# Two transformer blocks on one core: the value projections with 512-column matmuls into both accumulator banks

## The chip, the core and the metric

The kernel runs on one core of one Trainium2 chip. The metric is the device time of one launch in microseconds (us), from the first to the last instruction; lower is better. The core has a matrix engine (TensorE, PE in the profile, with a separate row PEld for its weight loads), a vector engine (VectorE, DVE), an activation engine (ScalarE, ACT), GpSimd (POOL), and SyncE (SP), which here only issues the DMAs of the weights and of input and output. Matmuls write their sums to PSUM, in banks of 128 partitions by 512 float32 values. Engines run their own instruction lists in order and wait for each other by semaphores.

## What is computed

One sequence of 256 tokens with 1024 features goes through two different blocks, all in float32. The first has block attention (8 heads of 64), gated linear attention (4 heads), and a gated feed-forward with a causal convolution; the second has a half-weighted feed-forward, two attentions (latent and chunked, 8 heads each), a gated merge, and another feed-forward. Cut to what bears on the change:

```python
proj = xn @ w_in[l]                                  # first block
mv = split_heads(proj[..., o_mv:o_gq], MOBA_HEADS)   # 512 columns of values
gv = split_heads(proj[..., o_gv:o_gr], GLA_HEADS)    # 512 columns of values
...
z = h @ w_in[l]                                      # second block
q_lat, kv_lat, k_pe_raw, ca_q, ca_k, ca_v, gate_a, gate_b = jnp.split(z, splits, axis=-1)
```

The three value projections `mv`, `gv` and `ca_v` (in the kernel `cav`) are each 256 tokens x 1024 features times 1024 x 512. Everything else that the kernel projects is needed with features on the partitions; the values are needed with tokens on the partitions, since attention sums over tokens.

## The kernel before

**Weights.** All weights arrive as one list of blocks of 128 x 1024 float32 (512 KB), called halves in the code; there are 282. SyncE loads half `h` into slot `h % 4` of `raw`. Each half is split into two float32r parts: ScalarE rounds it to `w_hi` (`hi`, L772), VectorE subtracts to get `w_lo` (`lo`, L1119). The activations `xn` are split alike into `xh` and `xl`. A product is then three matmuls: high x high, low x high, high x low. TensorE waits for `lo_ready` ahead of a half, and counts `half_used` up behind it; that count lets ScalarE overwrite the slot of the half four later, and tells it that a chunk of two halves is summed.

**Chunks.** A chunk is two halves, 256 weight columns by all 1024 features. It fills one PSUM bank. In the usual form (`feature_tile`, L355 to L357) the weights are the stationary operand and 256 tokens move. In the token form (`tokens_out=True`, L418 to L420) 128 tokens of `xh` or `xl` are stationary and 256 weight columns move; the two token halves fill the two halves of one bank. A half of either form is 24 matmuls of 256 columns. The token form is used for six chunks: 6 and 7 (`mv`), 8 and 9 (`gv`), `C_CAV` and `C_CAV + 1` (`cav`).

**Banks.** Chunks take PSUM banks 0 and 1 in turn (`bank_use(c)`). ScalarE empties a bank behind its chunk and counts `bank_free` up; TensorE waits for that count before it starts a new chunk in the bank. So one bank can be emptied while the next chunk fills the other.

**The order of the work.** Each engine's list is written out by hand. In the first block TensorE puts small pieces of attention between the halves: `rot` (rotary matmul), `level(l)` (one of nine steps of gated linear attention; it waits for `lv_q` from VectorE and `lv_k` from GpSimd, whose product is L298), `att_s`, `att_t`, `att_o` (scores, transposes, output of head pair `g`). From chunk 8 on, turn `g` of a loop runs the first half of chunk 8 + g, `att_s(g + 1)`, `att_t(g)`, `level(5 + g)`, the second half, `att_o(g)`. ScalarE's list in that turn is `hi` of a half, `att_pt`, `hi`, `att_exp(g + 1)`, `level_e`, `att_yh(g)` (L835, copies what `att_o` summed), and then the emptying of the chunk's bank (`vals`, L956, or `gr_evac`, L960).

In the second block TensorE runs a small projection into `v2` (L685 to L687; its two results lie in banks 1 and 0), then `C_CAV`, a rotary matmul (L704), `C_CAV + 1` with `s2(4)` (the scores of head pair 4) between its halves, and then eight chunks from `C_GATE` on with the attention pieces between the halves. ScalarE's list there: `hi` of `C_CAV`'s first half, the copy of `v2` from bank 1 (L1074), `hi` of the second half, the copy of `v2` from bank 0, `hi` of two halves, `vals` of `C_CAV`, `hi` of two halves, `att_exp(4)` (L826), `vals` of `C_CAV + 1`. `att_exp(4)` waits for `mask2(4)` on VectorE (L1274 to L1280), which waits for `s2(4)`.

`keep_clock` (L362) is a run of idle matmuls ahead of each norm's first chunk.

Of the kernel before, what the change touches and what calls it, by code (L numbers as in the profile page):

```python
# [19 lines left out]
P = 128  # L20
D = 1024
S = 256
KC = D // P
# [22 lines left out]
C_CAV = C_IN2 + 8  # L46
# [29 lines left out]
def build(nc, w, ada_w, x_in, cols_in, tab_in, gmask_in, glr_in, gup_in, bias_in, c_in, pos_in, out):  # L76
# [4 lines left out]
    ACT = mybir.ActivationFunctionType  # L81
# [3 lines left out]
    with ExitStack() as ctx:  # L85
# [114 lines left out]
        def slot(h):  # L200
            return h % NSLOT
# [150 lines left out]
        def _(pe):  # L352
# [11 lines left out]
            def feature_tile(u, h, kc, first, last):  # L364

                for f in range(2):
                    wc = slice((kc % 4) * 256 + f * P, (kc % 4) * 256 + f * P + P)
                    m = three(ps[:, u % 2, f * 256:f * 256 + 256], w_hi[:, slot(h), wc], w_lo[:, slot(h), wc],
                              xh[:, kc, :], xl[:, kc, :], first and f == 0, last)
                return m  # L370
# [26 lines left out]

            def chunk(c, i=0, tokens_out=False, halves=(0, 1)):

                ah, al = xh, xl  # L400
                u = bank_use(c)
                b = u % 2
                if halves[0] == 0 and not (isinstance(i, int) and u + 2 * i < 2):
                    pe.wait_ge(bank_free[b], u // 2 + i)
                for half in halves:
                    h = 2 * c + half
                    pe.wait_ge(lo_ready, h + 1 + 4 * i)
                    for k in range(4):
                        kc = 4 * half + k
                        first, last = half == 0 and k == 0, half == 1 and k == 3  # L410
                        if not tokens_out:
                            m = feature_tile(u, h, kc, first, last)
                            continue
                        for f in range(2):
                            a = slice(f * P, f * P + P)
                            wcol = slice(k * 256, k * 256 + 256)
                            o = ps[:, b, f * 256:f * 256 + 256]
                            pe.matmul(o, ah[:, kc, a], w_hi[:, slot(h), wcol], start=first and f == 0, stop=False, skip_group_check=True)  # L418
                            pe.matmul(o, al[:, kc, a], w_hi[:, slot(h), wcol], start=False, stop=False, skip_group_check=True)  # L419
                            m = pe.matmul(o, ah[:, kc, a], w_lo[:, slot(h), wcol], start=False, stop=last, skip_group_check=True)  # L420
                    m.then_inc(half_used, 1)
# [159 lines left out]
            level(1)  # L581
            chunk(6, tokens_out=True, halves=(0,))
            rot(5)
            level(2)
            chunk(6, tokens_out=True, halves=(1,))
            chunk(7, tokens_out=True, halves=(0,))
            level(3)
            chunk(7, tokens_out=True, halves=(1,))
            pe.wait_ge(rope_done, 4)
            att_s(0, b1["qT"], b1["kz"])  # L590
            level(4)
            for g in range(4):
                c = 8 + g
                chunk(c, tokens_out=c < 10, halves=(0,))
                if g < 3:
# [4 lines left out]
                else:  # L600
                    pe.wait_ge(lv_copied, 17)
                    evacuated(pe, 9)
                    for h in range(4):
# [5 lines left out]
                        if h % 2:  # L609
                            m.then_inc(go_full, 1)  # L610
                chunk(c, tokens_out=c < 10, halves=(1,))
                if g == 0:
# [87 lines left out]

            chunk(C_CAV, tokens_out=True, halves=(0,))
            evacuated(pe, bank_use(C_UQ) + 2)
            pe.wait_ge(pe_done, 1)
            pe.matmul(ps[:, 3, :], table("perm32", P), b2["qpr"][:, :], start=True, stop=True).then_inc(pe_rot, 1)  # L704
            chunk(C_CAV, tokens_out=True, halves=(1,))
            chunk(C_CAV + 1, tokens_out=True, halves=(0,))
            pe.wait_ge(pe_done, 2)
            evacuated(pe, bank_use(C_UQ) + 3)
            evacuated(pe, bank_use(C_UQ) + 4)
            s2(4)  # L710
            chunk(C_CAV + 1, tokens_out=True, halves=(1,))
            for c in range(8):
# [41 lines left out]
        def _(act):  # L754
# [198 lines left out]

            def vals(dst, c, cc):
                b = full(c)
                f(dst[:, :, cc * 256:cc * 256 + 256], bank2(b), ACT.Copy).then_inc(bank_free[b], 1)  # L956

# [5 lines left out]
            for c in range(2, 6):  # L963
                qraw(c)
                hi(c + 2)
                level_e(c - 2)
            vals(b1["mv"], 6, 0)
            hi(8)
            level_e(4)
            vals(b1["mv"], 7, 1)  # L970
            level_e(5)
            att_exp(0, sm1, st1)
            for g in range(4):
# [16 lines left out]
                if g == 3:  # L990
                    hi(C_OUT1 + 1, halves=(0,))
                if g < 2:
                    vals(b1["gv"], c, g)
                else:
                    gr_evac(c, g - 2)
# [79 lines left out]
            hi(C_CAV + 1)  # L1075
            vals(b2["cav"], C_CAV, 0)
            hi(C_GATE)
            att_exp(4, b2["sm2"], b2["st2"])
            vals(b2["cav"], C_CAV + 1, 1)
            for c in range(8):  # L1080
# [541 lines left out]
def _weights(a):  # L1622
# [11 lines left out]
    w = a["w_in"][0]  # L1634

    for c0, n in ((1536, 256), (1792, 256), (0, 512), (512, 512), (1024, 512), (2048, 512), (2560, 512)):
        for c in range(c0, c0 + n, 256):
            feature_chunk(w, r(c, c + 256))
# [17 lines left out]
    s.append(_padded(s[-1][:, :0]))  # L1656
    for c in range(1440, 4000, 256):
        feature_chunk(w, r(c, c + 256))
# [74 lines left out]
```

## Time and profile before

| what | before |
|---|---|
| device time, median of 3 runs | 1019.54 us (1017.79 to 1022.6) |
| span of the profiled execution | 1017.8 us |
| TensorE busy | 947.2 us (93%), 7412 matmuls |
| VectorE, ScalarE, GpSimd busy | 73%, 53%, 33% |
| the 288 matmuls of the value projections (L418 to L420) | 28.4, 27.1 and 27.1 us, about 283 ns each |
| DMA | 191.57 MB, mean 188 GB/s |

The profiled execution is one execution; its span stands beside the lowest of the three runs and 1.7 us under their median. A matmul's duration of about 283 ns covers its whole way through the engine; matmuls overlap, so their cost in a stream is the distance between the starts of two of them, which only the rows in order of time show. "Idle before" in a row is how long the engine had been without work, and the arrow names what ended it.

### The profile page before, as it was taken

The numbers are of one execution on the slowest core, as the hardware profiler recorded it, in microseconds if no ns is written. First come the engines' busy times: TensorE is split into PE (matmuls) and PEld (weight loads), VectorE is DVE, ScalarE is ACT, GpSimd is POOL, SyncE is SP. The second block draws the span as 40 slices with busy tenths as digits, with TensorE's granted clock in tenths as the row PEclk, the third lists the DMA queues.
The fourth block names the chain that finished last, engine by engine and source line by source line (L and its number), as shares of the span: only waits on it lengthen the run. The fifth ranks groups of instructions, "written<-read, shape, count | busy, mean of one in ns | idle before, by whom it ended". The sixth has DMA issues, their size and how long they took to land.

```text
span 1017.8 us, 20346 instructions
## 1 busy us (share of the span) xinstructions
PE 947.2 (93%) x7412; PEld 909.2 (89%) x7412; DVE 747.9 (73%) x942; ACT 539.5 (53%) x846; POOL 334.1 (33%) x267
## 2 busy tenths in 40 slices
PE   7999999888888986999997998999999999999996
PEld 5889998878888986899997997989999999999996
DVE  4589766999999666799999678666667575656444
ACT  4635566765656552665655455555554454343432
POOL 2053203656656883288656665000000000000000
PEclk9999999999999997999999899999999999999999
DMA  6443346767767775388886753553345546555651
GB/s 225 128 132 114 104 144 213 243 214 225 226 217 225 268 275 192 99 281 278 284 274 228 277 190 130 189 188 102 112 135 168 167 147 185 174 188 174 208 164 42
DMA packets 53228, 191.57 MB, mean 188 GB/s; under 512 B 5921, under 2 KB 6305, under 8 KB 53057
## 3 DMA queue, kind: packets, MB, share of 16 engines
q1 hardware_dynamic: 41760, 149.96, 45.1%
q0 software_dynamic: 10704, 39.46, 12.1%
q10 hardware_dynamic: 720, 1.54, 0.4%
q8 instruction: 31, 0.51, 0.2%
q14 instruction: 13, 0.10, 0.0%
HBM read 189.89 MB, written 1.05 MB: 188 GB/s over the span
## 4 chain that ended last, share of the span: by engine, by line
PE 64%; DVE 13%; issue 11%; POOL 5%; ACT 3%; DMA 1%; DVEq 1%; POOLq 0%; SPq 0%; ACTq 0%
PE ps L355 18%; PE ps L356 17%; PE ps L357 17%; POOL ada_mul L317 4%; DVE w_lo L1119 3%; PE ps L443 2%; PE ps L493 2%; DVE act_hi L1375 1%; DMA raw<-w 1%; PE ps L429 1%; DVE cv L1358 1%; DVE rstd L1124 1%; PE ps L418 1%; PE ps L419 1%; PE ps L420 1%
## 5 line engine op out<-in xcount | busy, mean ns | idle before, releaser
L355 PE MATMUL ps<-xh,w_hi 128*128 128x256 f32 x1472 | 424.8, 289 | 31.1 <-DVE w_lo L1119 21.3
L1119 DVE TENSOR_TENSOR w_lo<-raw,w_hi 128x1024 fp32r<-128x1024 f32 x282 | 368.1, 1331 | 116.2 <-ACT w_hi L772 115.9
L356 PE MATMUL ps<-xl,w_hi 128*128 128x256 f32 x1472 | 418.2, 284 | 0.0
L357 PE MATMUL ps<-xh,w_lo 128*128 128x256 f32 x1472 | 418.2, 284 | 0.0
L772 ACT ACTIVATE w_hi<-raw 128x1024 fp32r<-128x1024 f32 x282 | 286.7, 1052 | 76.2 <-PE ps L357 70.8
L355 PEld LDWEIGHTS ps<-xh,w_hi 128*128 128x128 f32 x1472 | 284.1, 193 | 41.0 <-DVE w_lo L1119 29.6
L356 PEld LDWEIGHTS ps<-xl,w_hi 128*128 128x128 f32 x1472 | 284.3, 193 | 0.3 <-issue 0.2
L357 PEld LDWEIGHTS ps<-xh,w_lo 128*128 128x128 f32 x1472 | 284.0, 193 | 0.0
L317 POOL TENSOR_TENSOR ada_mul<-ada_raw,cact 128x1024 f32<-128x1024 f32 x72 | 189.4, 2631 | 8.8 <-ACT cact L1010 8.8
L355 PE MATMUL ps<-act_hi,w_hi 128*128 (+1 forms) x528 | 153.1, 290 | 24.3 <-DVE w_lo L1119 24.3
L356 PE MATMUL ps<-act_lo,w_hi 128*128 (+1 forms) x528 | 150.9, 286 | 0.0
L357 PE MATMUL ps<-act_hi,w_lo 128*128 (+1 forms) x528 | 150.6, 285 | 0.0
L355 PEld LDWEIGHTS ps<-act_hi,w_hi 128*128 128x128 f32 x528 | 102.6, 194 | 26.0 <-issue 24.1
L356 PEld LDWEIGHTS ps<-act_lo,w_hi 128*128 128x128 f32 x528 | 102.7, 194 | 0.2
L357 PEld LDWEIGHTS ps<-act_hi,w_lo 128*128 128x128 f32 x528 | 102.4, 194 | 0.0
L1377 DVE TENSOR_TENSOR act_lo<-av,act_hi 128x256 f32 (+1 forms) x66 | 88.5, 1340 | 7.6
L310 POOL COPY mod<-ada_col 128x1 f32 (+1 forms) x72 | 55.5, 771 | 112.5 <-ACT ada_mul L878 112.3
L878 ACT ACTIVATE ada_mul<-ada_mul 128x1024 f32<-128x1024 f32 x72 | 75.5, 1049 | 28.3 <-POOL ada_mul L317 28.3
L869 ACT ACTIVATE sg<-ps 128x256 f32<-128x256 f32 x44 | 16.9, 383 | 123.5 <-PE ps L357 123.5
L303 POOL DMA_DIRECT2D ada_raw<-ada_w x72 | 42.3, 588 | 42.9 <-POOL ada_mul L317 41.6
L298 POOL TENSOR_TENSOR KL<-gkz,E 128x512 f32<-128x512 f32 x16 | 28.8, 1824 | 76.1 <-ACT E L847 76.1
L1375 DVE CAST act_hi<-av 128x256 f32 (+1 forms) x66 | 49.9, 755 | 0.0
(245 smaller groups left out, 1086.0 us busy)
## 6 DMA issues: line engine op xcount, KB each, us to landing
raw<-w SPq DMA_DIRECT2D x282, 512.0 KB, 4.3
ada_raw<-ada_w POOLq DMA_DIRECT2D x72, 512.0 KB, 4.1
X<-x_in SPq DMA_DIRECT2D x4, 256.0 KB, 5.8
bm<-bias_in POOLq DMA_DIRECT2D x1, 1024.0 KB, 5.2
out<-X SPq DMA_DIRECT2D x4, 256.0 KB, 2.2
tab<-tab_in ACTq DMA_DIRECT2D x1, 640.0 KB, 8.1
gmask<-gmask_in ACTq DMA_DIRECT2D x1, 512.0 KB, 10.2
cact<-c_in POOLq DMA_DIRECT2D x1, 512.0 KB, 5.1
```

The lines of the kernel that those rows point to most:

```text
L298: ins = pool.tensor_tensor(b1["KL"][:, l % 2, par, :, :], b1["gkz"][:, par, :, :], b1["E"][:, l % 2, :, :], ALU.mult)
L303: pool.dma_start(ada_raw[:, k, :], src).then_inc(ada_landed[k], 16)
L310: pool.tensor_copy(mod_cols[:, ds(n, 1)], ada_col[:, k:k + 1]).then_inc(ada_moved, 1)
L317: pool.tensor_tensor(ada_mul[:, k % 2, :], ada_raw[:, k, :], cact[:, :], ALU.mult).then_inc(ada_mult, 1)
L355: pe.matmul(o, lh, rh, start=start, stop=False, skip_group_check=True)
L356: pe.matmul(o, lh, rl, start=False, stop=False, skip_group_check=True)
L357: return pe.matmul(o, ll, rh, start=False, stop=stop, skip_group_check=True)
L772: f(w_hi[:, slot(h), :], raw[:, slot(h), :], ACT.Copy).then_inc(hi_ready, 1)
L878: f(ada_mul[:, n % 2, :], ada_mul[:, n % 2, :], ACT.Copy, accum_out=ada_col[:, n % 2:n % 2 + 1]).then_inc(ada_used, 1)
L1119: v.tensor_tensor(w_lo[:, slot(h), :], raw[:, slot(h), :], w_hi[:, slot(h), :].bitcast(F32), ALU.subtract).then_inc(lo_ready, 1)
L1375: v.tensor_copy(ah, av[:, vv, :]).then_inc(ah_done, 1)
L1377: v.tensor_tensor(al, av[:, vv, :], ah.bitcast(F32), ALU.subtract).then_inc(act_ready, 1)
```

## The change

The two chunks of a value projection become one piece of work, `wide(c, quarters)`. A half of its weights now holds two feature blocks (of 128) by 512 columns, not four by 256; the list of weights on the host is laid out so (`token_chunk`). A quarter is one such half: 12 matmuls of 512 columns, six for each token half, and token half `t` has a whole bank, `(bank_use(c) + t) % 2`. Both banks are filled throughout all four quarters. `wide` waits for both banks before its first quarter. The quarters stand where the four halves stood, with the same pieces of attention between them.

On ScalarE `vals(dst, c)` now empties both banks behind the fourth quarter, with two copies of 128 x 512. For `mv` it comes at the place of the second `vals`, and `hi(8)` and `level_e(4)` keep their order; for `gv` it comes in turn g = 1; for `cav` behind `att_exp(4)`.

```diff
+            def wide(c, quarters):
+                u = bank_use(c)
+                if quarters[0] == 0:
+                    for j in range(2):
+                        pe.wait_ge(bank_free[(u + j) % 2], (u + j) // 2)
+                for q in quarters:
+                    h = 2 * c + q
+                    pe.wait_ge(lo_ready, h + 1)
+                    for k in range(2):
+                        kc = 2 * q + k
+                        first, last = kc == 0, kc == KC - 1
+                        wcol = slice(k * 512, k * 512 + 512)
+                        for t in range(2):
+                            a = slice(t * P, t * P + P)
+                            o = ps[:, (u + t) % 2, :]
+                            pe.matmul(o, xh[:, kc, a], w_hi[:, slot(h), wcol], start=first, stop=False)
+                            pe.matmul(o, xl[:, kc, a], w_hi[:, slot(h), wcol], start=False, stop=False)
+                            m = pe.matmul(o, xh[:, kc, a], w_lo[:, slot(h), wcol], start=False, stop=last)
+                    m.then_inc(half_used, 1)
...
-            chunk(6, tokens_out=True, halves=(0,))
+            wide(6, (0,))
             rot(5)
             level(2)
-            chunk(6, tokens_out=True, halves=(1,))
-            chunk(7, tokens_out=True, halves=(0,))
+            wide(6, (1, 2))
             level(3)
-            chunk(7, tokens_out=True, halves=(1,))
+            wide(6, (3,))
...
-                chunk(c, tokens_out=c < 10, halves=(0,))
+                if g < 2:
+                    wide(8, (2 * g,))
+                else:
+                    chunk(c, halves=(0,))
...
-            chunk(C_CAV, tokens_out=True, halves=(0,))
+            wide(C_CAV, (0,))
...
-            chunk(C_CAV, tokens_out=True, halves=(1,))
-            chunk(C_CAV + 1, tokens_out=True, halves=(0,))
+            wide(C_CAV, (1, 2))
...
             s2(4)
-            chunk(C_CAV + 1, tokens_out=True, halves=(1,))
+            wide(C_CAV, (3,))
...
-            def vals(dst, c, cc):
-                b = full(c)
-                f(dst[:, :, cc * 256:cc * 256 + 256], bank2(b), ACT.Copy).then_inc(bank_free[b], 1)
+            def vals(dst, c):
+                full(c + 1)
+                for t in range(2):
+                    b = (bank_use(c) + t) % 2
+                    f(dst[:, t, :], ps[:, b, :], ACT.Copy).then_inc(bank_free[b], 1)
...
-            vals(b1["mv"], 6, 0)
             hi(8)
             level_e(4)
-            vals(b1["mv"], 7, 1)
+            vals(b1["mv"], 6)
...
-                if g < 2:
-                    vals(b1["gv"], c, g)
-                else:
+                if g == 1:
+                    vals(b1["gv"], 8)
+                elif g >= 2:
                     gr_evac(c, g - 2)
...
-            vals(b2["cav"], C_CAV, 0)
             hi(C_GATE)
             att_exp(4, b2["sm2"], b2["st2"])
-            vals(b2["cav"], C_CAV + 1, 1)
+            vals(b2["cav"], C_CAV)
```

Three places of the instruction lists follow. Line numbers of the changed kernel differ from those of the kernel before.

On TensorE, where `C_CAV` begins, behind the last three matmuls of the `v2` projection. Before:

```order
L685 MATMUL ps<-w_hi,cqh 128x512 [waits bank0_free]
L686 MATMUL ps<-w_hi,cql 128x512
L687 MATMUL ps<-w_lo,cqh 128x512
L418 MATMUL ps<-w_hi,xh 128x256 [waits lo_ready,bank1_free]
L419 MATMUL ps<-w_hi,xl 128x256
L420 MATMUL ps<-w_lo,xh 128x256
```

And in the changed kernel:

```order
L701 MATMUL ps<-w_hi,cqh 128x512 [waits bank0_free]
L702 MATMUL ps<-w_hi,cql 128x512
L703 MATMUL ps<-w_lo,cqh 128x512
L414 MATMUL ps<-w_hi,xh 128x512 [waits lo_ready,bank0_free,bank1_free]
L415 MATMUL ps<-w_hi,xl 128x512
L416 MATMUL ps<-w_lo,xh 128x512
```

The first matmul of the projection waited for bank 1 alone; now it waits for bank 0 too, which the `v2` matmuls right ahead of it have just filled.

On ScalarE, from the copies of `v2` to those of `cav` (`w_hi<-raw` is `hi` of one half, `sm2` with its sums `st2` is `att_exp(4)`). Before:

```order
L1074 ACTIVATE v2<-ps 128x512
L772 ACTIVATE w_hi<-raw 128x1024
L1074 ACTIVATE v2<-ps 128x512
L772 ACTIVATE w_hi<-raw 128x1024 x2
L956 ACTIVATE cav<-ps 128x2x256
L772 ACTIVATE w_hi<-raw 128x1024 x2
L826 ACT_TABLE_LOAD
L826 ACTIVATE sm2,st2<-sm2,st2 128x128 x2
L826 ACTIVATE sm2,st2<-sm2,st2 128x256 x2
L956 ACTIVATE cav<-ps 128x2x256
```

And in the changed kernel:

```order
L1091 ACTIVATE v2<-ps 128x512
L787 ACTIVATE w_hi<-raw 128x1024
L1091 ACTIVATE v2<-ps 128x512
L787 ACTIVATE w_hi<-raw 128x1024 x4
L841 ACT_TABLE_LOAD
L841 ACTIVATE sm2,st2<-sm2,st2 128x128 x2
L841 ACTIVATE sm2,st2<-sm2,st2 128x256 x2
L974 ACTIVATE cav<-ps 128x512 x2
```

The first copy of `cav` moved from ahead of the exponentials to behind them; both banks are now emptied there.

On ScalarE, from turn g = 0 to turn g = 1 of the loop in the first block (`yh1` is `att_yh`, `pt1` is `att_pt`). Before:

```order
L835 ACTIVATE yh1<-ps 128x256
L956 ACTIVATE gv<-ps 128x2x256
L772 ACTIVATE w_hi<-raw 128x1024
L831 ACTIVATE pt1<-ps 128x512
L772 ACTIVATE w_hi<-raw 128x1024
L826 ACTIVATE sm1,st1<-sm1,st1 128x128 x2
L826 ACTIVATE sm1,st1<-sm1,st1 128x256 x2
L845 ACTIVATE E<-E 128x512
L847 ACTIVATE E<-E 128x512
L835 ACTIVATE yh1<-ps 128x256
L956 ACTIVATE gv<-ps 128x2x256
```

And in the changed kernel:

```order
L850 ACTIVATE yh1<-ps 128x256
L787 ACTIVATE w_hi<-raw 128x1024
L846 ACTIVATE pt1<-ps 128x512
L787 ACTIVATE w_hi<-raw 128x1024
L841 ACTIVATE sm1,st1<-sm1,st1 128x128 x2
L841 ACTIVATE sm1,st1<-sm1,st1 128x256 x2
L860 ACTIVATE E<-E 128x512
L862 ACTIVATE E<-E 128x512
L850 ACTIVATE yh1<-ps 128x256
L974 ACTIVATE gv<-ps 128x512 x2
```

The copy at the end of turn 0 is gone, and the one at the end of turn 1 has become two.

## Rows read from the trace of the kernel before

**Rows 1.** The page: engine totals, and the granted TensorE clock in 40 slices.
```profile
PE 947.2 (93%) x7412; PEld 909.2 (89%) x7412; DVE 747.9 (73%) x942; ACT 539.5 (53%) x846; POOL 334.1 (33%) x267
PEclk9999999999999997999999899999999999999999
```
**Rows 2.** Stretches: us, busy time of each engine, clock, DMA share, GB/s.
```profile
68.00:110.00 42.00, 42.00 (x340) 39.91 (x340) 38.86 (x66) 22.73 (x49) 14.34 (x9) 1.00 0.29 93
674.00:790.00 116.00, 115.74 (x930) 110.06 (x930) 78.83 (x138) 62.12 (x128) 0.00 (x0) 1.00 0.43 140
```
**Rows 3.** TensorE in order of time: start, duration; 256 columns (first, last of 23), 512 (first, last of 5).
```profile
70.38 0.28 PE L419 MATMUL ps<-w_hi,xl 128*128 128x256 f32 x1
...
73.01 0.28 PE L420 MATMUL ps<-w_lo,xh 128*128 128x256 f32 x1
...
671.47 0.39 PE L686 MATMUL ps<-w_hi,cql 128*128 128x512 f32 x1
...
672.40 0.40 PE L687 MATMUL ps<-w_lo,cqh 128*128 128x512 f32 x1
```
**Rows 4.** TensorE and ScalarE at the starts of chunks 6 and 8.
```profile
70.18 0.36 PE L418 MATMUL ps<-w_hi,xh 128*128 128x256 f32 x1
...
67.82 0.60 ACT L952 ACTIVATE qraw<-ps 128x512 f32<-128x512 f32 x1 [5.20 <-PE ps L357]
...
89.45 0.36 PE L418 MATMUL ps<-w_hi,xh 128*128 128x256 f32 x1
...
86.55 0.60 ACT L956 ACTIVATE mv<-ps 128x512 f32<-128x512 f32 x1 [4.03 <-PE ps L420]
```
**Rows 5.** GpSimd's product for level 6, and TensorE's matmuls of level 6.
```profile
100.06 4.31 POOL L298 TENSOR_TENSOR KL<-gkz,E 128x512 f32<-128x512 f32 x2 [8.95 <-ACT E L847]
...
104.85 1.90 PE L493 MATMUL ps<-QL,KL 128*128 128x64 f32 x16
```
**Rows 6.** TensorE and ScalarE at the end of turn 1 and the start of chunk 10.
```profile
110.07 0.40 PE L469 MATMUL ps<-pt,mv 128*64 128x128 f32 x4
110.39 0.39 PE L355 MATMUL ps<-xh,w_hi 128*128 128x256 f32 x1
...
110.80 0.60 ACT L956 ACTIVATE gv<-ps 128x512 f32<-128x512 f32 x1
```
**Rows 7.** The start of C_CAV: TensorE, ScalarE, VectorE.
```profile
674.26 0.36 PE L418 MATMUL ps<-w_hi,xh 128*128 128x256 f32 x1 [1.46 <-DVE w_lo L1119]
...
674.32 0.59 ACT L1074 ACTIVATE v<-ps 128x512 f32<-128x512 f32 x1
...
672.89 1.22 DVE L1119 TENSOR_TENSOR w_lo<-raw,w_hi 128x1024 fp32r<-128x1024 f32 x1 [0.62 <-ACT w_hi L772]
```
**Rows 8.** From s2(4) to the first chunk of C_GATE: TensorE, ScalarE.
```profile
689.19 0.28 PE L420 MATMUL ps<-w_lo,xh 128*128 128x256 f32 x1
689.31 0.28 PE L355 MATMUL ps<-xh,w_hi 128*128 128x256 f32 x1
...
688.82 0.40 ACT L826 ACTIVATE sm<-sm,st 128x128 f32<-128x128 f32 x1 [3.89 <-DVE st L1280]
...
690.59 0.57 ACT L956 ACTIVATE cav<-ps 128x512 f32<-128x512 f32 x1
```
**Rows 9.** TensorE after idle stretches, and the clock granted after two of them.
```profile
178.88 0.39 PE L355 MATMUL ps<-xh,w_hi 128*128 128x256 f32 x1 [1.63 <-DVE w_lo L1119]
...
340.45 0.56 PE L355 MATMUL ps<-act_hi,w_hi 128*128 x1 [1.90 <-DVE w_lo L1119]
...
343.81 0.33 PE L355 MATMUL ps<-act_hi,w_hi 128*128 x1
...
178.90:182.30 3.40, 3.40 (x28) 3.40 (x29) 2.13 (x5) 3.40 (x10) 0.90 (x2) 1.00 0.88 289
340.40:343.80 3.40, 3.35 (x15) 3.35 (x16) 3.40 (x2) 1.90 (x2) 3.40 (x3) 0.51 0.75 264
```
**Rows 10.** All waits: engine, line <- what ended it: us in total, times, longest.
```profile
POOL cact L323 <- PE ps L357: 47.0, 1, 47.0
```

More of the change, by code:

```diff
@@ L396, in first_two, with chunk @@
                     m.then_inc(half_used, 1)
-            def chunk(c, i=0, tokens_out=False, halves=(0, 1)):
-                ah, al = xh, xl
+            def wide(c, quarters):
[17 more added lines that the diff above has]
+                    m.then_inc(half_used, 1)
+            def chunk(c, i=0, halves=(0, 1)):
                 u = bank_use(c)
@@ L410, in chunk @@
                         first, last = half == 0 and k == 0, half == 1 and k == 3
[L411 to L420, printed above, removed]
+                        m = feature_tile(u, h, kc, first, last)
                     m.then_inc(half_used, 1)
@@ L610, in _ @@
                             m.then_inc(go_full, 1)
-                chunk(c, tokens_out=c < 10, halves=(1,))
+                if g < 2:
+                    wide(8, (2 * g + 1,))
+                else:
+                    chunk(c, halves=(1,))
                 if g == 0:
@@ L1634, in _weights, with token_chunk @@
     w = a["w_in"][0]
+    def token_chunk(w, c):
+        s.extend([_tiles(w, k, 2, c) for k in range(0, KC, 2)])
     for c0, n in ((1536, 256), (1792, 256), (0, 512), (512, 512), (1024, 512), (2048, 512), (2560, 512)):
+        if c0 in (1024, 2048):
+            token_chunk(w, r(c0, c0 + 512))
+            continue
         for c in range(c0, c0 + n, 256):
@@ L1656, in _weights @@
     s.append(_padded(s[-1][:, :0]))
-    for c in range(1440, 4000, 256):
+    token_chunk(w, r(1440, 1952))
+    for c in range(1952, 4000, 256):
         feature_chunk(w, r(c, c + 256))
```

## The prediction

> **What bounds the kernel now.** I read the engine totals first [rows 1]: TensorE is busy 93% of the span, VectorE 73%. Then the two stretches in which the value projections lie [rows 2]: TensorE is busy for all 42.0 us of the first and 115.74 of 116.0 us of the second, at the full clock. The reader should see that an edit here is paid by TensorE's own list, matmul by matmul, and that each new wait on it is paid too. VectorE is close behind in the first stretch (38.86 of 42.0 us), so there a faster TensorE may run into it or into what it feeds. Last come the rows in order of time around each place where the change waits for a bank.
>
> **The matmuls.** 288 matmuls of 256 columns become 144 of 512. The 283 ns of one is no price, since they overlap; the starts are. At 256 columns, 23 starts take 73.01 - 70.38 = 2.63 us, 0.1195 us each. At 512 columns, in float32r with the same three products, the first and the last of five starts are 672.40 - 671.47 = 0.93 us apart, 0.2325 us each [rows 3]. Two narrow ones cost 0.239 to 0.240, one wide one 0.2325. So a wide one saves 0.007 us, a half of 24 narrow matmuls saves 12 x 0.007 = 0.085 us, and the 12 halves save 1.0 us in all. What the weight loads cost at either width is in these distances already, so their halved count brings nothing beyond that. That is the whole gain that the trace supports. The rest of the change is about when two banks must be free.
>
> The Trainium skill ("TensorE: Matmul & The Clock Gate", Back-to-back issue gap) puts a sustained stream of weight loads and matmuls at about 81 ns for 128 columns and 131 ns for 512. Interpolated to some 98 ns at 256, a pair would save about 65 ns, an estimate of 9.4 us for 144 pairs. The rows show 232.5 ns at 512 columns where that page has 131, so the sum goes by the rows.
>
> **Chunk 6, covered.** `wide(6)` needs the bank of chunk 5, which `qraw` empties from 67.82 to 68.42; TensorE comes at 70.18 [rows 4]. The matmuls of `rot` and `level(1)` hide it, with 1.8 us to spare. Nothing.
>
> **Chunk 8, covered.** `wide(8)` needs both banks of `mv`. The single copy ran at 86.55, for 0.60 us; a second one follows about 0.5 later and ends near 87.65, and TensorE comes at 89.45 [rows 4]. `att_s(0)` and `level(4)` hide it. Without them it would cost some 1.2 us. ScalarE has `level_e(5)` half a microsecond later, which TensorE needs only a whole half and two pieces of attention later.
>
> **Level 6, a part of the gain lost.** TensorE has saved seven halves, 0.60 us, when it comes to level 6, which began at 104.85. GpSimd's product for it ended at 100.06 + 4.31 = 104.37 [rows 5]; it starts from VectorE's and ScalarE's chain, which is not moved. With 0.10 for the semaphore TensorE can start at 104.47, so only 0.38 of the 0.60 remain. With the eighth half the first block's gain is 0.46 us.
>
> **Chunk 10, a new wait.** Chunk 10 used the bank that `vals` had emptied a turn earlier. Now it is emptied in turn 1, behind `att_yh(1)`, which waits for `att_o(1)`, the work right ahead of chunk 10. The copy ran from 110.80 to 111.40 [rows 6]. From a finished release to the first matmul I take 0.14 us, from the start of `C_CAV` (674.12 to 674.26, [rows 7]). So chunk 10 starts at 111.54, not at 110.39: 1.15 us, all on TensorE, with chunk 11, the output projection and everything behind queued after it. The second copy delays `hi` of a half that TensorE needs a half and some attention later: nothing. First block: +1.15 - 0.46 = **+0.7 us**.
>
> **C_CAV, a longer wait.** Before, TensorE waited here 1.46 us for `w_lo` (672.89 + 1.22). Now it needs the second copy of `v2` too, which stands behind `hi` of a half and ends at 674.32 + 0.59 = 674.91; with 0.14 the start is 675.05, not 674.26 [rows 7]: **+0.8 us**. `w_lo` of the later halves stays ahead.
>
> **C_GATE, the largest wait.** TensorE ended the projection and went on at 689.31 without a stop, since that bank had been emptied ahead of the exponentials. Now both copies stand behind `att_exp(4)`, and that waits for VectorE's mask, which waits for `s2(4)`. `s2(4)` moves by 0.79 for `C_CAV`'s late start and back by three halves, 0.25: +0.54. The exponentials ran from 688.82 to 690.59, and a copy takes 0.57 [rows 8]. So the first bank is free at 690.59 + 0.54 + 0.57 = 691.70, and TensorE goes on at 691.84, not 689.31: +2.5 us, which holds the +0.8 of `C_CAV` and the gain of the four halves (0.34) in it. Behind it wait the eight gate chunks with all attention, and through them the rest. If the exponentials ran before TensorE was done, the cost would be one copy and a semaphore, 0.7 in place of about 2.1; they can't, since `s2(4)` has to come ahead of them. Second block: **+2.5 us**.
>
> The Trainium skill ("Perfetto Trace Analysis", Matmuls) says that independent groups should rotate through the banks, so that the emptying of one overlaps the next, and also that larger matmuls are more efficient. The change trades the first for the second. By the rule alone each of the five starts would pay a copy, about 0.6 us, so 3.0 in all; the rows put two of them at nothing and one at over 2.
>
> **The clock.** TensorE's idle stretches get longer. An idle stretch of 1.63 us was followed by a full clock; one of 1.90 was followed by one of half speed (0.51, 1.2 of 2.4 GHz) until 343.81 [rows 9]. There the 16 starts from 340.45 on took 3.36 us, where the full clock takes 16 x 0.12 = 1.92: 1.45 us lost. After the change TensorE is idle from 672.80 (672.40 + 0.40, [rows 3]) to 675.05, 2.25 us, longer than the row that lost its clock, and from about 689.9 to 691.8, 1.9 us, which equals it. I take one loss of the two: **+1.45 us**; the ends are none and 2.9.
>
> **The sum.** +0.7 + 2.5 + 1.45 = +4.65 us. Does any of it get hidden later? The one long chain apart from TensorE's is GpSimd's modulation product, and it starts from a TensorE matmul behind the first new wait [rows 10]; all norms start from TensorE too. So it stays. Against the profiled execution, 1017.8 + 4.65 = 1022.5; that execution stands at the low end of the three runs, and for the median I take 1019.54 + 4.65 = **1024.2 us**.
>
> **The rivals.**
> Both stretches lose the clock (slower by over 0.5%). The place is the same, the price a second 1.45 us, and it decides from an idle stretch between 1.63 and 1.90 us on: +6.1, 1025.6. For it: both idle stretches reach 1.90. Against: one equals it only just, and the idle ends are worked out to a tenth at best.
> No clock is lost: +3.2, 1022.7. For it: the only row of this length is a single one.
> The waits cost nothing (faster, or the same). That would be so if TensorE's delay ran into a later wait that didn't move, as at level 6. The 1.0 or 0.7 us gain is left: 1018.6. Against: TensorE idles 0.26 us in the 116 us behind `C_CAV` [rows 2].
> The wide matmul is much cheaper than its five starts show, because those stood in a run of six only. The bound is that it costs one narrow start: 144 x 0.12 = -17 us; halfway, and less the waits, about 1012. Against: the four distances are equal to a hundredth. The skill's figures above are this rival.
> The change doesn't do what it says: the lists show 512 columns and both waits, so I give that nothing.
>
> **How the numbers follow.** One clock loss 0.36, both 0.24, none 0.24, waits hidden wholly or for the most part 0.10, cheap wide matmul 0.02, the rest for what I have not seen. The range 1019.8 to 1026.6 takes the first three with 1 us either way for the runs' own spread. A measurement of this kernel tells about 0.5%, 5.1 us, from no change, which is 1024.6. Slower: both losses and some 0.3 of the single one, 0.36. Faster: 0.04, the cheap matmul with a little more. Same: 0.60.
>
> **What would show it.** In the changed profile: wide starts 0.2325 apart; no idle stretch ahead of chunks 6 and 8; one of about 1.1 us ahead of chunk 10, released by a `gv` copy; 2.2 ahead of `C_CAV`, released by a `v2` copy; 1.9 ahead of `C_GATE`, released by a `cav` copy behind the exponentials; half clock behind one of the last two. I am wrong if starts are under 0.22, if the copy ahead of `C_GATE` comes before the exponentials, or if the difference at 690 is not found again at the end.

## The result, and the profile after

| what | before | changed |
|---|---|---|
| device time, median | 1019.38 us (1017.72 to 1022.6, 20 runs) | 1022.99 us (1019.86 to 1026.81, 20 runs) |
| ratio to before | | 1.0036, 95% interval 1.0024 to 1.0048 |
| span of the profiled execution | 1017.8 us | 1024.4 us |
| matmuls | 7412 | 7268 |

The changed kernel is 3.7 us slower (2.4 to 4.9), inside the half per cent that was called no change. One run of the kernel before, of 1144.2 us at a mean clock of 0.75, is left out of everything below. Line numbers below are those of the changed kernel, or of the kernel that is named.

The page of the changed kernel has TensorE's busy time up by 1.4 us, though it has 144 matmuls fewer, and the clock row has other notches than before [rows 1]:

```profile
PE 948.6 (93%) x7268; PEld 903.6 (88%) x7268; DVE 751.6 (73%) x942; ACT 539.4 (53%) x846; POOL 333.3 (33%) x267
...
PEclk8989999999999998999998999999999999999998
```

The list of all waits of TensorE (us in total, times, longest) names the new ones:

```profile
PE ps L414 <- ACT v L1091: 2.2, 1, 2.2
...
PE ps L355 <- ACT cav L974: 1.8, 1, 1.8
...
PE ps L355 <- ACT gv L974: 1.0, 1, 1.0
...
PE ps L504 <- DVE AT L1357: 0.3, 1, 0.3
```

The first three are ahead of `C_CAV`, `C_GATE` and chunk 10. The fourth, ahead of level 3, was not forecast. In order of time, with the idle time before each and what ended it:

```profile
84.34 1.97 PE L504 MATMUL ps<-QL,KL 128*128 128x64 f32 x16 [0.30 <-DVE AT L1357]
...
113.80 0.39 PE L355 MATMUL ps<-xh,w_hi 128*128 128x256 f32 x1 [0.98 <-ACT gv L974]
...
677.75 0.47 PE L414 MATMUL ps<-w_hi,xh 128*128 128x512 f32 x1 [2.21 <-ACT v L1091]
...
694.33 0.54 PE L355 MATMUL ps<-xh,w_hi 128*128 128x256 f32 x1 [1.85 <-ACT cav L974]
```

The last three answer to [rows 6 to 8], where `C_CAV` alone waited, for 1.46 us. The wide matmuls themselves, in the second and third quarter of `cav`, the first and the last of 21 starts:

```profile
682.13 0.40 PE L414 MATMUL ps<-w_hi,xh 128*128 128x512 f32 x1
...
686.70 0.40 PE L416 MATMUL ps<-w_lo,xh 128*128 128x512 f32 x1
```

20 distances in 4.57 us are 0.2285 us each, against 0.2325 in [rows 3] and 0.239 for two narrow ones. That is the price inside a stream; what a whole quarter saves comes with the experiments.

**Where the 6.6 us between the two profiled executions lie.** Both traces are cut at the same starts of TensorE: the first matmul of chunk 6, of chunk 10, of the `v2` projection, of `C_CAV`, of `C_GATE`, and of the transposes of head pair 4.

| stretch | before | changed | difference |
|---|---|---|---|
| start to chunk 6 | 70.18 | 72.91 | +2.73 |
| chunk 6 to chunk 10 | 40.21 | 40.89 | +0.68 |
| chunk 10 to `v2` | 560.77 | 560.10 | -0.67 |
| `v2` to `C_CAV` | 3.10 | 3.85 | +0.75 |
| `C_CAV` to `C_GATE` | 15.05 | 16.58 | +1.53 |
| `C_GATE` to the transposes | 5.50 | 7.10 | +1.60 |
| transposes to the end | 322.99 | 322.97 | -0.02 |

The first row can't come from the change, which begins at chunk 6. There and in the third row the two executions differ in where the clock was at half speed. The three rows of the change itself, 0.68 + 0.75 + 1.53 = **2.96 us**, are the banks and the matmuls. The sixth row is the clock behind the wait for `cav`:

```profile
677.80:681.00 3.20, 3.20 (x13) 2.48 (x14) 2.99 (x3) 1.85 (x2) 0.00 (x0) 1.00 0.79 221
694.30:697.60 3.30, 3.27 (x15) 3.27 (x16) 1.98 (x5) 1.41 (x2) 0.00 (x0) 0.52 0.00 0
```

(Stretch, length, busy time of PE, PEld, DVE, ACT, POOL, granted clock, DMA share, GB/s.) Behind the 2.21 us wait the clock stayed at 2.4 GHz, behind the 1.85 us wait it was at 1.2 GHz.

### The profile page after: what moved, and what is told of

Same layout as the page of the kernel before. It is cut to its first block, busy times and chain, and to the rows that moved or that the text cites. A ratio compares the mean times of both kernels' runs of the same rounds, so it can differ in the third digit from the quotient of the medians.

```text
span 1024.4 us, 20055 instructions
## 1 busy us (share of the span) xinstructions
PE 948.6 (93%) x7268; PEld 903.6 (88%) x7268; DVE 751.6 (73%) x942; ACT 539.4 (53%) x846; POOL 333.3 (33%) x267
## 4 chain that ended last, share of the span: by engine, by line
PE 65%; DVE 14%; issue 12%; POOL 4%; ACT 3%; DMA 1%; DVEq 1%; POOLq 0%; SPq 0%; ACTq 0%
PE ps L355 18%; PE ps L356 18%; PE ps L357 18%; POOL ada_mul L317 3%; DVE w_lo L1135 2%; PE ps L454 2%; PE ps L440 1%; PE ps L504 1%; DVE cv L1374 1%; DVE rstd L1140 1%; DVE cv L1371 1%; DMA raw<-w 1%; ACT w_hi L787 1%; DVE av L1379 1%; DVE act_hi L1391 1%
## 5 line engine op out<-in xcount | busy, mean ns | idle before, releaser
L1393 DVE TENSOR_TENSOR act_lo<-av,act_hi 128x256 f32 (+1 forms) x66 | 94.9, 1438 | 7.6
L1386 DVE TENSOR_TENSOR av<-sg,ps 128x256 f32<-128x256 f32 x44 | 18.3, 416 | 39.8 <-ACT sg L884 39.5
```

The lines of the kernel that those rows point to most:

```text
L1393: v.tensor_tensor(al, av[:, vv, :], ah.bitcast(F32), ALU.subtract).then_inc(act_ready, 1)
```

## The experiments

Since one execution differs from the next by where its clock falls, I read three things of each kernel: the stretches between the starts above, from its profile; the ratio to the kernel before; and the difference at equal clock. For the last, 246 runs (each has its time and its mean granted clock) were fitted with one slope and one level per kernel; the slope is 0.59 us for 0.001 of the clock. Its intervals are 95%, but the runs come from several chips: with a level for each chip as well, the values move by up to 0.5 us (cav_bank2 to +0.4, mv_copy_first to +0.3, all_four to -0.5). Nor does equal clock take out all that the clock costs. By estimate, a loss of 3.2 us at half speed lowers the mean clock of a run by 0.0016, which the slope values at 0.9 us, where the traces below have it cost 1.5 to 1.6. So a kernel that often loses its clock behind a wait keeps a part of that price in the last column.

| kernel | chunk 6 to 10 | `v2` to `C_CAV` | `C_CAV` to `C_GATE` | ratio (95%) | at equal clock, us |
|---|---|---|---|---|---|
| before | 40.21 | 3.10 | 15.05 | 1 | 0 |
| changed | 40.89 | 3.85 | 16.58 | 1.0036 (1.0024 to 1.0048) | +4.0 ± 0.4 |
| mv_only | 40.19 | 3.10 | 15.05 | 1.0005 (0.999 to 1.0021) | +0.3 ± 0.5 |
| gv_only | 40.84 | 3.09 | 15.05 | 1.0 (0.9985 to 1.0015) | +0.8 ± 0.5 |
| cav_only | 40.20 | 3.84 | 18.17 (clock lost) | 1.0021 (1.0006 to 1.0036) | +2.6 ± 0.5 |
| all_three | 39.80 | 3.00 | 14.72 | 0.9987 (0.9972 to 1.0002) | -0.9 ± 0.5 |
| gv_first | 39.80 | 3.84 | 16.58 | 1.0039 (1.0022 to 1.0056) | +2.4 ± 0.5 |
| cav_first | 40.88 | 3.85 | 16.99 (clock lost) | 1.0025 (1.0006 to 1.0043) | +2.4 ± 0.5 |
| cav_bank2 | 40.87 | 3.00 | 14.70 | 0.9995 (0.9978 to 1.0013) | +0.8 ± 0.5 |
| longer | 40.89 | 3.85 | 18.97 (clock lost) | 1.0043 (1.0024 to 1.0063) | +5.3 ± 0.6 |
| mv_copy_first | 40.20 | 3.10 | 15.05 | 0.9987 (0.9968 to 1.0005) | -0.1 ± 0.5 |
| before_copy_first | 40.22 | 3.10 | 15.05 | 0.9997 (0.9976 to 1.0017) | -0.2 ± 0.5 |
| all_four | 39.78 | 3.00 | 14.70 | 0.9995 (0.9978 to 1.0011) | -1.0 ± 0.5 |

The theory under test: the loss is three waits for banks, one ahead of chunk 10, two around `cav`, and the clock behind the longer ones. Its rivals: the wide matmuls cost something of their own; or one of the two blocks makes the loss alone.

### One projection at a time

```diff
 mv_only (gv and cav as before):
-                if g < 2:
-                    wide(8, (2 * g,))
-                else:
-                    chunk(c, halves=(0,))
+                chunk(c, tokens_out=c < 10, halves=(0,))
...
-            wide(C_CAV, (0,))
+            chunk(C_CAV, tokens_out=True, halves=(0,))
```

The other quarters, the copies of ScalarE and the layout of the weights go back in the same way; in gv_only and cav_only it is the other two projections that do.

> Only the mv projection is wide; gv and cav stay as two chunks. Theory of the waits: no idle stretch of TensorE ahead of chunks 6 and 8, four quarters 0.085 us shorter each, so -0.3 us against the kernel before. Rival (wide matmuls themselves bring a cost that the waits don't show): TensorE is idle ahead of chunk 6 or 8, or the stretch from chunk 6 to chunk 8 is not shorter.

> Only the gv projection is wide. Theory of the waits: TensorE is idle about 1.0 us ahead of chunk 10, released by the copy of gv; level 6 is not held, since only three quarters are saved ahead of it; +1.15 - 0.34 = +0.8 us. Rival (the wait is made up by a later one): the idle stretch is there, but the time from chunk 10 to the first norm is shorter by as much.

> Only the cav projection is wide. Theory of the waits: idle stretches of 2.2 us ahead of C_CAV and 1.9 ahead of C_GATE, +2.5 us from L685 to C_GATE, and in most executions one or two losses of the clock of 1.45 us, so +2.5 to +5.4, about +3.5 in the median. Rival (the first block's waits make the loss): under +1.5.

gv_only and cav_only have the waits that were expected, at slightly lower prices. gv_only loses 40.84 - 40.21 = 0.63 us (0.8 expected), with 0.98 us of idle ahead of chunk 10. cav_only's ratio is 2.1 us (0.6 to 3.7), under the 2.5 to 5.4 that were expected. It loses 0.74 ahead of `C_CAV`, and then has both waits, with the clock lost behind the first this time and kept behind the second:

```profile
675.45 0.67 PE L414 MATMUL ps<-w_hi,xh 128*128 128x512 f32 x1 [2.21 <-ACT v L1100]
675.92 0.63 PE L415 MATMUL ps<-w_hi,xl 128*128 128x512 f32 x1
676.35 0.63 PE L416 MATMUL ps<-w_lo,xh 128*128 128x512 f32 x1
...
693.62 0.38 PE L355 MATMUL ps<-xh,w_hi 128*128 128x256 f32 x1 [1.85 <-ACT cav L978]
693.85 0.28 PE L356 MATMUL ps<-xl,w_hi 128*128 128x256 f32 x1
693.97 0.28 PE L357 MATMUL ps<-xh,w_lo 128*128 128x256 f32 x1
```

Starts 0.43 us apart at the first place are half speed; 0.12 at the second is full speed. `C_CAV` to `C_GATE` took 18.17 us here and 16.58 where the clock stayed: 1.59 us for one loss. At equal clock the three parts add up to 0.3 + 0.8 + 2.6 = 3.7 us, the changed kernel has 4.0. So two thirds of the loss are `cav`; by the stretches it is 2.28 of 2.96 us, three quarters.

mv_only did not give its gain: 40.19 us, where 39.9 was expected. Its trace has TensorE held ahead of level 3, not by a bank of chunks, but by VectorE's copy of level 2 (`level_copy(2)`, L1366 there):

```profile
83.50 0.74 PE L513 MATMUL ps<-QL,KL 128*128 128x64 f32 x5 [0.31 <-DVE AT L1366]
```

So what failed is not the banks. There was no idle ahead of chunks 6 and 8, as the theory had it, but chunk 6 to chunk 8 took 19.26 us against 19.27 before: not shorter, which was the second of the rival's two signs. Whether wide matmuls cost something of their own, as the rival said, or VectorE takes the gain, mv_only alone can't tell; the experiments below can.

### The waits taken away

all_three:

```diff
+                if g == 1:
+                    vals(b1["gv"], 8)
                 att_yh(g, yh1, g)
...
-                    for j in range(2):
+                    for j in range(2 if c != C_CAV else 0):
                         pe.wait_ge(bank_free[(u + j) % 2], (u + j) // 2)
...
-                            o = ps[:, (u + t) % 2, :]
+                            o = ps[:, 2 if c == C_CAV and t == 0 else (u + t) % 2, :]
+                            if c == C_CAV and kc == 0 and t == 1:
+                                pe.wait_ge(bank_free[(u + 1) % 2], (u + 1) // 2)
```

ScalarE copies `cav`'s first half from bank 2 without counting `bank_free`, and its first copy of `v2` counts two, since bank 1 then stays free. cav_bank2 has these edits without the first one, gv_first has the first one alone.

> All three projections wide, with the waits taken away: the copies of gv stand ahead of att_yh(1); token half 0 of cav is summed in bank 2, which is free there, so that C_GATE finds its bank empty, and the wait for bank 0 stands ahead of the first matmul of token half 1. Theory of the waits: no idle stretch ahead of chunk 10 and C_GATE, 1.5 ahead of C_CAV as before; -0.7 to -1.0 us against the kernel before, so 1018.5 or so. Rival (wide matmuls cost something of their own, or the clock falls in any case): it stays at +1 or more.

> The changed kernel with token half 0 of cav in bank 2 and the wait for bank 0 ahead of the first matmul of token half 1; gv as in the changed kernel. Theory: no idle ahead of C_GATE, 1.5 ahead of C_CAV; against the kernel before only the first block's +0.7 is left, less 0.34: +0.4 us. Rival: the stretch behind C_CAV still is longer than before.

> The changed kernel with the copies of gv ahead of att_yh(1) on ScalarE; all else alike. Theory: the first copy runs while TensorE is in att_o(1), so the 1.0 us of idle ahead of chunk 10 shrinks to under 0.2, and nothing else moves: 1.0 us less than the changed kernel. Rival (att_yh(1), now 1.1 us later, is waited for): the same time turns up ahead of a later matmul of attention.

In their stretches all three came out by the theory. all_three takes 39.80, 3.00 and 14.72 us where the kernel before takes 40.21, 3.10 and 15.05: 0.84 us less. (0.10 of that is a start of `C_CAV` that comes sooner behind the same release; no row says why.) The time agrees: -0.9 us at equal clock, while the ratio, 0.9987 (0.9972 to 1.0002), doesn't exclude no change. With all_four below, this is the fastest form of the change, by a gain that can only just be told.

The quarters show what the wide form saves where it stands. The four halves of `gv` took 11.99 us before and 11.54 in all_three, those of `cav` 12.16 and 11.84. The saving is 0.45 and 0.32 us, about 0.1 per quarter and not the 12 x (0.239 - 0.2285) = 0.13 of the long stream: in a quarter by itself the starts are 0.23 apart. The last quarter of `cav`, before and in all_three, the first two starts and the gate's:

```profile
686.25 0.47 PE L418 MATMUL ps<-w_hi,xh 128*128 128x256 f32 x1
686.55 0.28 PE L419 MATMUL ps<-w_hi,xl 128*128 128x256 f32 x1
...
689.31 0.28 PE L355 MATMUL ps<-xh,w_hi 128*128 128x256 f32 x1
...
685.12 0.58 PE L416 MATMUL ps<-w_hi,xh 128*128 128x512 f32 x1
685.54 0.39 PE L417 MATMUL ps<-w_hi,xl 128*128 128x512 f32 x1
...
688.08 0.28 PE L355 MATMUL ps<-xh,w_hi 128*128 128x256 f32 x1
```

The quarter took 3.06 and 2.96 us; behind the first distance, 11 wide ones take 2.54 us, 0.231 each. So the wide form has no cost of its own that would eat the gain, and the gain is there once nothing waits.

In cav_bank2 TensorE goes from `cav` to the gate chunks without a stop:

```profile
691.77 0.39 PE L418 MATMUL ps<-w_lo,xh 128*128 128x512 f32 x1
692.00 0.28 PE L355 MATMUL ps<-xh,w_hi 128*128 128x256 f32 x1
...
693.39 0.57 ACT L976 ACTIVATE cav<-ps 128x512 f32<-128x512 f32 x1
```

The copy ends at 693.96, two microseconds behind the gate's first matmul, and nobody waits. cav_bank2 keeps only the first block's loss. Its stretches add up to 0.66 - 0.10 - 0.35 = +0.2 us where +0.4 was expected; at equal clock it is +0.8 ± 0.5, and its ratio, 0.9995, shows no difference. In gv_first the copies ran ahead of `att_yh`, the first of them while TensorE was in `att_o(1)`, and chunk 6 to chunk 10 fell from 40.89 to 39.80. The time behind it, chunk 10 to the output projection, is 21.98 us in gv_first and 21.97 in the changed kernel, so the later `att_yh` is waited for by no one. Its ratio, 1.0039, is not under the changed kernel's; two kernels measured apart are told from each other to 0.2% at best, and at equal clock it is 1.6 us lower.

### The order of the copies around the exponentials, and a longer wait

```diff
 cav_first:
-            att_exp(4, b2["sm2"], b2["st2"])
             vals(b2["cav"], C_CAV)
+            att_exp(4, b2["sm2"], b2["st2"])
...
 longer:
             att_exp(4, b2["sm2"], b2["st2"])
+            f(b2["th"][:, 0:4, :], b2["bm"][:, 0:4, :], ACT.Copy)
             vals(b2["cav"], C_CAV)
```

> The changed kernel with the copies of cav ahead of att_exp(4); all else alike. Theory: TensorE waits for one copy and a semaphore ahead of C_GATE, some 0.7 us and not 1.85, and the exponentials end 1 us later, which transpose 4 doesn't need yet: 1.2 us less than the changed kernel, and no clock loss at C_GATE, up to 1.45 more in executions that had one. Rival (the exponentials are late then): an idle stretch ahead of the transposes of head pair 4.

> The changed kernel with one more copy of 128 x 1024 on ScalarE (into a tile that is overwritten later) between att_exp(4) and the copies of cav. Theory: the wait ahead of C_GATE is on the path in full, so it grows from 1.85 to 2.9 us and the time by 1.05, and at 2.9 us idle the clock falls behind it in nearly every execution, which adds some 0.7 in the median: +1.0 to +2.5 against the changed kernel. Rival (delays here are made up later): less than 0.5.

cav_first: the idle ahead of `C_GATE` fell from 1.85 to 0.69 us:

```profile
687.91 0.39 PE L355 MATMUL ps<-xh,w_hi 128*128 128x256 f32 x1 [0.69 <-ACT cav L974]
```

`C_CAV` to `C_GATE` is 16.99 us, against 18.17 in cav_only; both lost the clock behind `C_CAV`. That is 1.18 us less, as expected, and `C_GATE` to the transposes is 5.59 us, so the late exponentials are hidden. longer: the idle grew to 2.79 us, and the stretch to 18.97, 0.80 more than cav_only's (`cav`'s last quarter with the wait behind it took 5.91 us against 4.96, 0.95 more; the loss of clock in the first quarter cost 0.14 less). The clock was lost behind both waits, and the transposes came 7.09 us behind `C_GATE` instead of 5.6. At equal clock it is 1.3 us over the changed kernel, by the ratios 0.7. The delay is not made up. So the wait ahead of `C_GATE` is paid in full, and what sets its length is the row of work that stands between `s2(4)` and the copy.

### What holds mv's gain

```diff
 mv_copy_first (mv_only with), before_copy_first (before with), all_four (all_three with):
+            level_copy(2)
             level_d(4)
-            level_copy(2)
```

> Only mv wide, as in mv_only, and on VectorE level_copy(2) stands ahead of level_d(4). In mv_only TensorE was idle 0.31 us ahead of level 3, released by that copy, and the stretch from chunk 6 to chunk 10 was 40.19 us against 40.21 before. Theory (VectorE's copy takes the gain of mv): the copy ends 0.6 us earlier, the idle stretch is gone and chunk 6 to chunk 10 takes 39.85 to 39.9. Rival (wide quarters of mv save nothing there for another reason): 40.2 with no idle stretch, or the wait turns up at level 4.

> The kernel before with the same two VectorE instructions swapped and nothing wide. Theory: the copy hardly held TensorE there, so chunk 6 to chunk 10 takes 40.1 to 40.2 and the time is the same. Rival (the swap is worth something by itself): 39.9 or less.

> All three projections wide, the three waits taken away as in all_three, and the swap on VectorE. Theory: chunk 6 to chunk 10 takes 39.45 to 39.5 (39.80 in all_three), and the whole is 1.0 to 1.4 us under the kernel before at equal clock. Rival (level 6 holds it now, by GpSimd's product): 39.7 to 39.8, with an idle stretch ahead of level 6.

The copy that held level 3 came earlier, and that wait went. But the gain did not come: 40.20 us, and the wait is at level 4 now, for VectorE's next copy, as the rival said. all_four shows the same, 39.78 us with no wait at level 6, so neither of the two forecasts for that stretch holds; its -1.0 ± 0.5 us at equal clock is just at the edge of the 1.0 to 1.4 that were expected. On VectorE in mv_copy_first:

```profile
86.27 1.97 PE L513 MATMUL ps<-QL,KL 128*128 128x64 f32 x16 [0.48 <-DVE AT L1366]
...
79.04 0.76 DVE L1366 COPY_PREDICATED AT<-gmask,ps 128x256 f32<-128x256 int32 x2
79.71 0.69 DVE L1337 TENSOR_TENSOR E<-G 128x512 f32<-128x512 f32 x1
80.31 2.36 DVE L1144 TENSOR_TENSOR w_lo<-raw,w_hi 128x1024 fp32r<-128x1024 f32 x2
82.58 1.52 DVE L1343 TENSOR_TENSOR QL<-gq,E 128x256 f32<-128x256 f32 x1
84.03 1.76 DVE L1337 TENSOR_TENSOR E<-G 128x512 f32<-128x512 f32 x1
85.71 0.75 DVE L1366 COPY_PREDICATED AT<-gmask,ps 128x256 f32<-128x256 int32 x2
```

and around level 4, where VectorE's busy time is the third figure behind the length:

```profile
82.00:90.00 8.00, 7.52 (x51) 6.65 (x50) 7.96 (x11) 3.88 (x11) 5.96 (x4) 1.00 0.37 131
```

VectorE is busy for 7.96 of 8.0 us around level 4. In this stretch its list is as long as TensorE's, so whatever TensorE saves on `mv` it waits for at the next level. Which level that is depends on the order; the sum does not. All thirteen kernels show it, wide or narrow, swapped or not: VectorE's copy of level 3 starts 16.90 to 16.93 us behind the start of chunk 6, level 4 on TensorE 17.47 to 17.50, and chunk 6 to chunk 8 takes 19.25 to 19.28 us. The copy, in the kernel before (chunk 6 at 70.18) and in mv_only (at 72.07):

```profile
87.10 0.76 DVE L1341 COPY_PREDICATED AT<-gmask,ps 128x256 f32<-128x256 int32 x2
...
88.98 0.76 DVE L1366 COPY_PREDICATED AT<-gmask,ps 128x256 f32<-128x256 int32 x2
```

The kernel before stood at that edge already: chunk 6 to chunk 10 is 40.21 there and 40.22 with the swap. And it is not the wide form that costs `mv` its gain: in all_four its second and third quarter, with no wait among them, took 5.55 us against 5.84 for the same halves in before_copy_first, and level 3 began 10.97 us behind chunk 6 against 11.35. Level 4 began at 17.49 and 17.50: the gain was there, and was waited for.

## Why the prediction was right, point by point

**The waits, found and placed.** All three were where the prediction had them, released by what it named. Chunks 6 and 8 had no idle ahead of them.

**The clock.** Taken: one loss of 1.45 us. A loss costs 1.59 behind `C_CAV` and 1.50 behind `C_GATE` (7.10 - 5.60), so the price was near. How often it happens was read from one row, and there the forecast was too high for the median: of the 3.7 us, 2.96 are the three stretches, so about 0.7 (-0.6 to +1.9) is left for the clock. In the five profiles that have both waits (changed, cav_only, gv_first, longer, and cav_first, whose second wait is only 0.69), a 2.2 us wait lost the clock in three and kept it in two; a 1.85 us wait lost it in one of three; the 2.79 us wait lost it. An idle stretch of this length loses the clock in some executions and not in others. Both ends of the range, none and two, do occur: gv_first had none, longer had both.

**The matmuls.** Forecast 0.085 us per half, from 0.2325 us a start. The long stream in the middle of `cav` has 0.2285, but the quarters of the changed kernel that stand alone have 0.229 to 0.238 behind their first distance, with [rows 3]'s 0.2325 in the middle. The quarters of `gv` and `cav` save 0.77 us in eight, 0.10 each, so this term held. The rival of a much cheaper matmul is out: it saved 0.0105 us, not 0.12. (That rival's 1012 us left out most of the waits: 1019.5 - 8.6 for the matmuls + 1.15 + 2.9 for the waits is some 1015.)

**Level 6.** This step of the prediction failed. TensorE was to be held by GpSimd's product there; it was held by VectorE's copy at level 3, and chunk 6 to chunk 8 kept its length to 0.01 us. So all of `mv`'s gain was lost, 0.5 us by its quarters in all_four, and not 0.2. TensorE began level 3 11.43 us behind chunk 6 in the changed kernel and 11.44 before, level 4 17.48 and 17.49: it was held at both. The sign stood in the trace of before: VectorE busy for 38.86 of 42.0 us [rows 2], which the prediction read and then followed up at the wrong engine.

**Chunk 10.** Forecast +1.15 for the wait. From the end of `gv`'s last quarter to chunk 10 the changed kernel took 1.86 us and the kernel before 0.80, so the wait cost 1.06. The 0.1 less is the release: the first copy ended at 113.75 (113.16 + 0.59), TensorE went on at 113.80, 0.05 later and not 0.14. The block's sum of +0.7 was met at 0.68 partly by luck: a gain of 0.40 from `gv` alone stood in for the 0.46 of both projections, and the wait was 0.09 short.

**C_CAV.** Forecast +0.8, measured 0.75. **C_GATE.** Forecast +2.5 with `C_CAV`'s part in it, measured 0.75 + 1.53 = 2.28. The chain from `s2(4)` to the first exponential is 5.00 us both before (683.82 to 688.82) and after. In the changed kernel, TensorE and ScalarE:

```profile
686.93 0.38 PE L454 MATMUL ps<-nz,qn 128*128 128x128 f32 x2
...
691.93 0.40 ACT L841 ACTIVATE sm<-sm,st 128x128 f32<-128x128 f32 x1 [5.11 <-DVE st L1296]
...
693.70 1.05 ACT L974 ACTIVATE cav<-ps 128x512 f32<-128x512 f32 x2
```

What was a little off is the release: by the 0.57 us of a copy in [rows 8] the first one ended at 694.27, and TensorE went on at 694.33, 0.06 later and not 0.14; and `s2(4)` stood 9.18 us behind `C_CAV` and not 9.56, so three quarters gave back 0.38 and not 0.25.

**The total.** Forecast +4.65 us and 1024.2; measured 3.7 us and 1022.99. The banks and matmuls came to 2.96 where 3.2 was said; the rest of the difference is the clock's share, which these runs only bound. Against the profiled execution the forecast was a span of 1022.5; it had 1024.4, 2.7 us of it ahead of chunk 6. The rival in which the waits cost nothing is out by cav_bank2 and longer. The mechanism and the places of all three bank waits were right; that the total fell so near also owes something to one clock loss having been counted where the median shows about half of one.

The Trainium skill's rule to rotate through the banks ("Perfetto Trace Analysis", Matmuls) is borne out here: the wide form took 2.28 us too much for `cav` until its first half had a bank of its own; in all_three, where it had one, the same two stretches are 0.43 us shorter than before.

## What to carry to other kernels

A form that fills two banks at once gives up the one that was being emptied: count the start of every piece of work behind it, and read from the copying engine's list what stands ahead of the copy, since that, and not the copy, sets the price. If a bank is free for the while, use it; if not, put the copy ahead of whatever else the copying engine waits for. And look for the second-busiest engine of the stretch before counting on a gain: where it is full, the gain turns into a wait.

## What the hardware showed

A float32r matmul of 512 columns costs 0.2285 us in a stream and one of 256 columns 0.1195, so doubling the width saves 4% of a pair, no more. In runs of 12 with other work on both sides the wide starts are 0.229 to 0.238 apart in the changed kernel, and the saving is some 0.1 us of 3.0.

The clock can fall some time after the work has come back. In cav_first it was still full for the first starts behind the wait and then fell:

```profile
670.92 0.47 PE L414 MATMUL ps<-w_hi,xh 128*128 128x512 f32 x1 [2.21 <-ACT v L1091]
671.22 0.39 PE L415 MATMUL ps<-w_hi,xl 128*128 128x512 f32 x1
671.45 0.39 PE L416 MATMUL ps<-w_lo,xh 128*128 128x512 f32 x1
671.68 0.51 PE L414 MATMUL ps<-w_hi,xh 128*128 128x512 f32 x1
671.99 0.63 PE L415 MATMUL ps<-w_hi,xl 128*128 128x512 f32 x1
```

The spread of the runs is mostly the clock. Among the 96 runs of the kernel before, those with a mean clock of 0.988 took 1015.0 to 1016.0 us, those with 0.981 took 1019.0 to 1021.3. A difference of 1 us between two kernels is hidden in that unless runs are compared at equal clock, or stretches in the traces.

VectorE's subtraction of 128 x 512 (L1337) took 0.69 us at 79.71 and 1.76 us at 84.03 in mv_copy_first. The second began beside GpSimd's product (81.81 to 85.24), the first did not. In mv_only the same instruction came behind the product's end at 88.18 and took 0.68. The other traces bear this out. In the thirteen of them the 13 rows of this instruction that began inside such a product took 1.76 to 1.78 us and ended 0.53 to 0.56 us behind its end. The 52 beside no product took 0.66 to 0.69, and so did the 13 that began up to 0.1 us ahead of one. No experiment moved the product on purpose. The swap gained nothing by this either way: in mv_only the product fell on the pair of `w_lo` subtractions, which took 3.43 us and not 2.36 (80.31 in mv_copy_first).

```profile
81.81 3.43 POOL L298 TENSOR_TENSOR KL<-gkz,E 128x512 f32<-128x512 f32 x2 [5.37 <-ACT E L866]
...
83.58 3.43 DVE L1144 TENSOR_TENSOR w_lo<-raw,w_hi 128x1024 fp32r<-128x1024 f32 x2
84.41 3.77 POOL L298 TENSOR_TENSOR KL<-gkz,E 128x512 f32<-128x512 f32 x2 [4.70 <-ACT E L866]
```
